# Reordering the S5 rows, dt's chain, the convolution state and GELU in a one-core decoder step

## The reference

```
xn   = rmsnorm(x)
z, xbc, dt_raw, u = split(xn @ w_in)
xbc  = silu(causal_conv4(xbc));  new conv state = last 3 input rows
dt   = softplus(dt_raw + dt_bias)
y    = SSD(xbc, dt, A) in chunks of 128;  new SSM state (16 heads x 64 x 128), per sample too
y1   = rmsnorm(y * silu(z))
s5   = diagonal complex SSM on u in 64 groups of 16 channels (state 64)
s    = gelu(s5);  y2 = rmsnorm(s * sigmoid(s @ w_glu + b))
x    = x + concat(y1, y2) @ w_out
x    = x + moe(rmsnorm(x))      # 32 experts, top 2 of one group of 8
out  = rmsnorm(x)
```

## Time and profile before

| | us |
|---|---|
| median of 3 runs | 1015.04 (1013.79 to 1019.23) |
| the profiled execution | 1019.88 |
| its span | 1018.0 |
| TensorE busy | 922.2 (91%) |
| VectorE busy | 491.6 (48%) |
| ScalarE busy | 306.4 (30%) |
| GpSimd busy | 227.7 (22%) |

### The profile page before, as it was taken

How to read it: one execution, slowest core, us unless ns; L and a number is a source line. 1 busy time by engine, 2 the same in 40 slices (tenths; PEclk the granted TensorE clock), 3 DMA queues, 4 the chain that set the end, 5 groups by cost and what they waited for, 6 DMA issues and landing times.

```text
span 1018.0 us, 16758 instructions
## 1 busy us (share of the span) xinstructions
PE 922.2 (91%) x6345; PEld 672.0 (66%) x6345; DVE 491.6 (48%) x856; ACT 306.4 (30%) x641; POOL 227.7 (22%) x468
## 2 busy tenths in 40 slices
PE   8999999989998999999989999999999888788870
PEld 7889878878896688999864555555555444445440
DVE  6999997254545888965352222222222221221136
ACT  3025322263323776423321121212212111111224
POOL 0100788888510111000001111111111101101103
PEclk9999989899999899999999999999999999999995
DMA  7576063033359755657599999989999999999976
GB/s 280 129 144 100 22 118 101 23 106 103 117 119 238 232 186 195 214 175 266 198 405 391 423 423 426 390 329 426 424 423 425 421 427 423 422 428 421 423 295 252
DMA packets 88356, 281.56 MB, mean 277 GB/s; under 512 B 37312, under 2 KB 56720, under 8 KB 70488
## 3 DMA queue, kind: packets, MB, share of 16 engines
q1 hardware_dynamic: 77632, 253.96, 67.0%
q0 software_dynamic: 8480, 19.60, 5.9%
q10 hardware_dynamic: 2176, 7.04, 1.9%
HBM read 266.39 MB, written 23.58 MB: 285 GB/s over the span
## 4 chain that ended last, share of the span: by engine, by line
PE 58%; DMA 20%; DVE 15%; issue 3%; ACT 2%; SPq 1%; POOL 0%; POOLq 0%; ACTq 0%; DVEq 0%
DMA sb_arena<-w_up 16%; PE ps L720 16%; PE ps L974 9%; PE ps L1111 8%; PE ps L1095 8%; PE ps L1086 7%; DVE sb_arena L1517 6%; PE ps L1045 2%; DMA sb_arena<-ssm_in 2%; DVE sb_arena L1526 1%; PE ps L812 1%; DVE sb_arena L2094 1%; DVE sb_arena L1650 1%; DVE sb_arena L1642 1%; DMA sb_kxf<-x_scr,sb_tok_of 1%
## 5 line engine op out<-in xcount | busy, mean ns | idle before, releaser
L720 PE MATMUL ps<-sb_arena 128*128 128x260 f32 (+2 forms) x1152 | 269.0, 395 | 2.5 <-DVE sb_arena L1551 2.3
L720 PEld LDWEIGHTS ps<-sb_arena 128*128 128x128 f32 x1152 | 222.4, 195 | 49.5 <-issue 6.4
L1111 PE MATMUL ps<-sb_arena 128*64 128x512 f32 x544 | 127.6, 612 | 18.4 <-DVE sb_arena L2094 18.4
L1095 PE MATMUL ps<-sb_arena 128*64 128x256 f32 x1088 | 123.9, 380 | 14.1 <-DMA sb_arena<-w_up 14.1
L1086 PE MATMUL ps<-sb_arena 128*64 128x256 f32 x1088 | 123.9, 380 | 10.7 <-issue 10.7
L2090 DVE TENSOR_TENSOR sb_s5b<-sb_s5b,ps 128x256 f32<-128x256 f32 x36 | 22.4, 623 | 219.8 <-PE ps L1095 219.1
L1086 PEld LDWEIGHTS ps<-sb_arena 128*64 128x64 f32 x1088 | 83.3, 137 | 61.2 <-issue 32.5
L662 POOL DMA_INDIRECT out_scr<-sb_kxf,sb_rwc x36 | 35.7, 992 | 389.8 <-DVE sb_kxf L2107 388.9
L1095 PEld LDWEIGHTS ps<-sb_arena 128*64 128x64 f32 x1088 | 78.6, 137 | 55.6 <-DMA sb_arena<-w_up 19.6
L1491 ACT ACTIVATE sb_kxf<-ps,sb_gate_of 64x512 f32<-64x512 f32 x36 | 24.5, 682 | 264.6 <-PE ps L1111 264.5
L1111 PEld LDWEIGHTS ps<-sb_arena 128*64 128x64 f32 x544 | 37.5, 139 | 86.6 <-issue 59.9
(11 more groups left out here) (326 smaller groups left out, 1142.6 us busy)
## 6 DMA issues: line engine op xcount, KB each, us to landing
sb_arena<-w_gate SPq DMA_DIRECT2D x32, 2048.0 KB, 24.2
sb_arena<-w_up SPq DMA_DIRECT2D x31, 2048.0 KB, 27.4
sb_arena<-w_down SPq DMA_DIRECT2D x31, 2048.0 KB, 23.4
sb_arena<-wi SPq DMA_DIRECT2D x27, 512.0 KB, 4.3
sb_arena<-w_out SPq DMA_DIRECT2D x16, 512.0 KB, 4.2
sb_arena<-cs_scr ACTq DMA_DIRECT2D x4, 1024.0 KB, 4.9
sb_arena<-ssm_in POOLq DMA_DIRECT2D x8, 512.0 KB, 9.3
sb_arena<-wglu SPq DMA_DIRECT2D x8, 512.0 KB, 5.4
```

The lines of the kernel that those rows point to most:

```text
L720: last = mm(ps[:, b0 + h, 0:t1 - t0], ring[w % 3][:, k, :], src[:, k, t0:t1], start=k == 0, stop=k == KD - 1)
L1095: last = mm(ps[64 * r:64 * r + 64, 1, 0:256], xt[:, k, :], Wu[i][:, k, 256 * r:256 * r + 256], start=k == 0, stop=k == KD - 1)
L1111: last = mm(ps[64 * r:64 * r + 64, 4, :], ht[:, k % 2, 64 * (k // 2):64 * (k // 2) + 64], Wd[j][:, k, 512 * r:512 * r + 512], start=k == 0 ...
```

## The change

- `y_store`: SyncE stores the even j and the samples, a new `y_store_odd` on ScalarE the odd j, in chunk 3: half 0 ahead of segment_exp(3), half 1 behind b_tokens(3).
- GpSimd starts the loads of samples 4 to 7 only after the store of half 0 has landed, and the broadcast and the loads of samples 0 and 1 only after the store of half 1.
- wide(13) stands ahead of L795; dt's polynomial is cut into pieces with conv(5), conv(6) and conv(7) in between; ScalarE's exponentials for it come after conv_silu(3).
- `ncp` and `ncs` are copied by ScalarE in `raw_evac`, from PSUM; the DMA of both waits for raw_done.
- `bc_scr`'s store is issued after raw_evac(16). conv_silu(10) goes ahead of decays(0), conv_silu(11) ahead of segment_exp(0).
- ds (`dts`, `eA`, `xds`) is computed ahead of the S5 sample states.
- GELU of tile i waits for `xn_free` i + 1, which wide(27) gives tile by tile; tiles 0 to 3 come ahead of z_evac(27) and sample_decay(0), tiles 4 to 7 behind it.
- sample_c(0) and (1) come after st_ev of chunk 3, sample_update(0) and (1) ahead of the masks of chunk 4, sample_c(2) to (5) after them.

```
             def y_store(half):
                 sp.wait_ge(y5_ev, 8 * half + 8)
                 gs = slice(32 * half, 32 * half + 32)
-                for j in range(J):
+                for j in range(0, J, 2):
                     sp.dma_start(ydst[j][:, gs], Ug[16 * j:16 * j + 16, gs, 0:NC5]).then_inc(y5_st[half], 16)
...
             pl.wait_ge(y5_mm, 8)
+            pl.wait_ge(y5_st[0], 16 * 9)
             for b in range(4, NS):
                 pl.dma_start(h0b[b], hin[b]).then_inc(h0s_ld[1], 16)
...
             pl.wait_ge(s5_out, 32)
+            pl.wait_ge(y5_st[1], 16 * 9)
             pl.dma_start(bcf, bc_scr.rearrange("b c -> (b c)").partition_broadcast(P)).then_inc(bc_ld, 16)
...
             pl.wait_ge(h0s_ld[0], 32)
-            pl.wait_ge(y5_st[1], 16 * 9)
...
+                    if w == 27 and k < KD - 1:
+                        last.then_inc(xn_free, 1)
...
             wide(12)
+            wide(13)
             pe.wait_ge(dt_ev, 1)
...
             last.then_inc(dtt_mm, 1)
-            wide(13)
             wide(14)
...
                 sm = dst[:, 531:563].rearrange("p (b j) -> p b j", j=CONV)
-                act_(sm[:, :, 3], ps[:, b0 + 1, SPLIT:N - SPLIT], ACT.Copy).then_inc(wide_free[w % 2], 1)
+                act_(sm[:, :, 3], ps[:, b0 + 1, SPLIT:N - SPLIT], ACT.Copy)
                 f = conv_tile(i)
+                act_(ncp[:, f, :], ps[:, b0 + 1, SPLIT - 3:SPLIT], ACT.Copy)
+                act_(ncs[:, f], ps[:, b0 + 1, SPLIT:N - SPLIT], ACT.Copy).then_inc(wide_free[w % 2], 1)
...
             conv_silu(9)
+            conv_silu(10)
             decays(0)
+            conv_silu(11)
...
             segment_exp(0)
-            conv_silu(XBC - 2)
-            conv_silu(XBC - 1)
...
+            def y_store_odd(half):
+                ac.wait_ge(y5_ev, 8 * half + 8)
+                gs = slice(32 * half, 32 * half + 32)
+                for j in range(1, J, 2):
+                    ac.dma_start(ydst[j][:, gs], Ug[16 * j:16 * j + 16, gs, 0:NC5]).then_inc(y5_st[half], 16)
...
             for c in range(4):
+                if c == 3:
+                    y_store_odd(0)
                 if c:
                     segment_exp(c)
                 b_tokens(c)
+                if c == 3:
+                    y_store_odd(1)
                 ac.wait_ge(l_exp, 4 * c + 4)
                 spread(c + 1)
...
-            sample_decay(0)
-            sample_decay(1)
-            z_evac(27)
-            b_tokens(4)
-            segment_exp(4)
-            for i in range(8):
...
+            for i in range(4):
+                gelu(i)
+            z_evac(27)
+            sample_decay(0)
+            for i in range(4, 8):
+                gelu(i)
+            sample_decay(1)
+            b_tokens(4)
+            segment_exp(4)
...
-            for m in (15, 13, 11, 9, 7, 5, 3):
+            for m in (15, 13):
                 tt(sp_u, sp_u, spz, ALU.mult)
                 ts(sp_u, sp_u, 1.0 / m, None, ALU.add)
+            conv(6)
+            for m in (11, 9, 7, 5, 3):
+                tt(sp_u, sp_u, spz, ALU.mult)
+                ts(sp_u, sp_u, 1.0 / m, None, ALU.add)
+            conv(7)
...
+                if c == 4:
+                    for b in range(2):
+                        sample_update(b)
                 for g in range(2):
                     dv.wait_ge(l_exp, 4 * c + 2 * g + 2)
...
-                for b in ((), (), (), (0, 1), (2, 3, 4, 5))[c]:
-                    sample_c(b)
+                if c == 4:
+                    for b in range(2, 6):
+                        sample_c(b)
                 dv.wait_ge(y_mm, c + 1)
...
                 if c == 3:
                     for b in range(2):
-                        sample_update(b)
+                        sample_c(b)
```

More of the change, by code:

```diff
@@ L306, in build @@
         raw_done, conv_done, silu_done = sem("raw_done"), sem("conv_done"), sem("silu_done")
-        h_done, sst_done, y5_mm, y5_ev = sem("h_done"), sem("sst_done"), sem("y5_mm"), sem("y5_ev")
+        xn_free = sem("xn_free")
+        h_done, y5_mm, y5_ev = sem("h_done"), sem("y5_mm"), sem("y5_ev")
         y5_st = [sem(f"y5_st{i}") for i in range(2)]
@@ L356, in build @@
         NW = 36
+        ydst = y_scr[:, 0:NP_].rearrange("(g c) (j m) -> j c g m", c=C5, j=J)
+        ysdst = y_scr[:, NP_:N].rearrange("(g c) b -> c g b", c=C5)
         def wide_bank(w):
@@ L439, in _ @@
                 ring_load(w)
-            sp.wait_ge(conv_done, XBC)
+            sp.wait_ge(raw_done, XBC)
             sp.dma_start(a["o_conv_p"].rearrange("p (k j) -> p k j", k=XBC), ncp[:]).then_inc(outs, 16)
@@ L1223, in _ @@
             conv_silu(2)
+            raw_evac(13)
+            conv_silu(3)
             ac.wait_ge(s5_dve, 3)
@@ L1234, in _ @@
             raw_evac(15)
+            conv_silu(5)
+            raw_evac(16)
             ac.wait_ge(bcs_ev, 2)
             ac.dma_start(bc_scr, btf[16:24]).then_inc(bc_st, 16)
-            conv_silu(5)
-            raw_evac(16)
             conv_silu(6)
@@ L1319, in _, with gelu @@
                         decays(c + 1)
-            sample_decay(0)
-            sample_decay(1)
-            z_evac(27)
-            b_tokens(4)
-            segment_exp(4)
-            for i in range(8):
+            def gelu(i):
                 if i % 4 == 0:
                     ac.wait_ge(yraw_ld[i // 4], 16)
+                if i < 7:
+                    ac.wait_ge(xn_free, i + 1)
+                else:
+                    ac.wait_ge(wide_done, 28)
                 act_(yg[:, i, META:NP_].rearrange("p (m j) -> p j m", j=J),
@@ L1669, in conv @@
                     stt(dst[:, 0:NP_], src[:, k:k + NP_], w_[k], dst[:, 0:NP_], ALU.mult, ALU.add)
-                    stt(dst[:, NP_:N], sm[:, :, k], w_[k], dst[:, NP_:N], ALU.mult, ALU.add)
-                link(V.tensor_copy(ncp[:, f, :], src[:, NP_:NP_ + 3]))
-                V.tensor_copy(ncs[:, f], sm[:, :, 3]).then_inc(conv_done, 1)
+                    last = V.scalar_tensor_tensor(dst[:, NP_:N], sm[:, :, k], w_[k], dst[:, NP_:N], ALU.mult, ALU.add)
+                    if k < CONV - 1:
+                        link(last)
+                last.then_inc(conv_done, 1)
             for s_ in range(2):
@@ L1698, in _ @@
             V.tensor_tensor(sp_u, sp_u, dvf, ALU.min).then_inc(s5_dve, 1)
+            conv(5)
             dv.wait_ge(s5_act, 5)
@@ L1739, in _ @@
                 conv(i)
+            dv.wait_ge(ds_mm, 1)
+            link(V.tensor_copy(dts[:], ps[:, 6, 256:256 + 64].rearrange("p (i b) -> p i b", i=8)))
+            tt(eA[:], dts[:], bc(aexp[:], 2, NS), ALU.mult)
+            ts(eA[:], eA[:], -1.0, None, ALU.mult)
+            dv.wait_ge(silu_done, XBC)
+            V.tensor_tensor(xds[:], dts[:], xcX[:, :, NP_:N], ALU.mult).then_inc(ds_ev, 1)
             lo, hi = slice(0, 64), slice(64, 128)
@@ L1748, in _ @@
             tt(smp[hi], bc(Aj[lo, 1, 1], 1, NS), h0v[lo], ALU.mult)
-            V.tensor_tensor(sst[:], sst[:], smp, ALU.add).then_inc(sst_done, 1)
-            dv.wait_ge(ds_mm, 1)
-            link(V.tensor_copy(dts[:], ps[:, 6, 256:256 + 64].rearrange("p (i b) -> p i b", i=8)))
-            tt(eA[:], dts[:], bc(aexp[:], 2, NS), ALU.mult)
-            ts(eA[:], eA[:], -1.0, None, ALU.mult)
-            dv.wait_ge(silu_done, XBC)
-            V.tensor_tensor(xds[:], dts[:], xcX[:, :, NP_:N], ALU.mult).then_inc(ds_ev, 1)
+            V.tensor_tensor(sst[:], sst[:], smp, ALU.add).then_inc(s5_dve, 1)
             def sample_c(b):
```

9 lines of the change are left out of this document (1 added, 8 removed).

## The result

Ten runs of the changed kernel had a median of 1024.92 us (1022.45 to 1027.65), ten of the kernel before 1017.15 (1013.79 to 1022.35): ratio 1.0073, 95% interval 1.0049 to 1.0097. The prediction, 1014 with a range of 1003 to 1022, was wrong. The profiled execution took 1022.66, with a span of 1020.9 (before 1019.9 and 1018.0). The forecast stood on 1015.04, the median of three runs; ten gave 1017.15, so 2.1 of the 10.9 us between forecast and result are the base.

What follows compares the result with a forecast made beforehand. TensorE's waits ahead of the expert phase and slow clock behind them, at most some 21 us, were taken as the bound. 0.0 - 3.4 + 2.5 + 0.0 = -0.9, put on the median 1015.04: 1014; range 1003 to 1022, eight in ten.

Steps and rivals of the forecast that it cites:

- (a): dt in pieces, wide(13) ahead of the dt products: dt wait goes, wide(16) waits 3.0; 0.0 us, ends -2.5 and +0.8.
- the signs: For (a): L795 without a wait, a new wait of 2 to 3.5 us before wide(16), released by the weight load.
- (d): The rest: ncp and ncs copies on ScalarE, earlier convolution outputs, ScalarE's store issues; together 0.0 us.
- (b): ds before S5 sample states, two SiLUs earlier: ds wait goes, 2.1 us wait before wide(21); -3.4 us, between -5.1 and -1.7.
- (c): S5 rows, GELU, sample states: the 4.9 us wait only moves into wide(28); +2.5 us, ends -7.7 and +8.6.
- Y: Time when all S5 stores have landed, after which POOL issues broadcast and first state loads: 322.5 us, was 335.
- The first states behind Y: POOL's broadcast and two loads, issued at Y, take 14 us and land at 336.5, between 328.5 and 341.
- Behind the fifth tile of wide(28): Extra time in the last chunk: 1.5 us for slow clock, 0.5 for wide(34)'s bank freed late.
- R2: Slower: POOL's broadcast behind the second half bounds the fifth tile of wide(28); +7.7 us in all, 1023; chance 0.15.
- R3: ScalarE sits in store issues, spread(4) lands at 330, z_evac(27) at 340; +4, so +2.9 in all, 1018; chance 0.10.

Runs made afterwards that it cites:

- e12: The changed kernel with (a) and (b) taken back, (c) and (d) kept: 1031.34 us, ratio 1.0143 to the kernel before.
- e2: The changed kernel with GELU 4 to 7 ahead of sample_decay(0) on ScalarE: 1023.93 us, ratio 1.0087 to the kernel before.
- e6: e5 with POOL's loads of states 4 to 7 behind the stores of half 1: 1009.49 us, ratio 0.9931 to the kernel before.
- e11: e6 with SyncE alone issuing all S5 stores, ScalarE none: 1012.27 us, ratio 0.9940 to the kernel before.
- e1: The changed kernel with (c) taken back, (a), (b) and (d) kept: 1011.18 us, ratio 0.9956 to the kernel before.
- e10: e6 with z_evac(20) alone ahead of segment_exp(0): 1012.86 us, ratio 0.9944 to the kernel before.
- e3: The changed kernel with spread(4) ahead of the second four stores on ScalarE: 1024.33 us, ratio 1.0093 to the kernel before.
- e4: The changed kernel with POOL's order as before, broadcast and states 0 and 1 not waiting for the stores: 1017.84 us, ratio 1.0026.
- e5: The changed kernel with the edits of e3 and e4 together: 1010.73 us, ratio 0.9936 to the kernel before.
- e9: e8 with ScalarE's wait for bcs_ev and its bc_scr store behind the sixteen evacuations of the lower-triangle products: 1015.8 us, ratio 0.9982.
- e13: e9 with ssd_c(2) ahead of all S5 output products: 1002.3 us, ratio 0.9862 to the kernel before.
- the kernel with more of the front: e1 with wide(16)'s weight load ahead of the last Toeplitz copies and z_evac(20) ahead of segment_exp(0): 1021.02 us, ratio 1.0036.
- e8: e6 with wide(16)'s weight load ahead of the last Toeplitz copies and z_evac(20) ahead of segment_exp(0): 1020.46 us, ratio 1.0027.

## Why the prediction was wrong, step by step

**(a), dt in pieces: the signs came, the cause is in part (d).** The wait at dt went, and one of 2.05 us came before wide(16), released by the weight load as named; 3.0 was forecast. From the blocks ahead of the raw dt (109.64 and 110.69) to the lower-triangle products the kernel now takes 58.4 us against 60.0, so 1.6 gained, between the ends of the range (-2.5 and +0.8), against 0.0 taken: the new wait is 1 us shorter, and the clock fell behind it for about 3.4 us instead of 6.8. But e12 shows that (d) alone takes the wait at dt away, with 56.7 us for the same stretch. Against that the kernels with (a) take 56.1 to 57.2 where the clock stayed full behind wide(16)'s wait (e2 to e6, e11), and 58.3 to 58.8 where it fell (e1, the changed kernel, e10): on top of (d), (a) is worth nothing that can be told.

**(b), ds earlier: right in mechanism.** The wait of 4.2 went and one of 1.83 was born before wide(21), released by z_evac(20); forecast 2.1. Between the lower-triangle products and wide(21) 5.3 us were gained, and 1.2 more inside wide(21), at 7.25 instead of 8.47. That is 6.5 in the profile against -3.4. The clock stayed full in the gap, which is the end named as -5.1; the other 1.4 are luck, the shorter stretch of slow clock near 190 us, which the step does not touch. Over many runs (a), (b) and (d) together gave -4.5 (the interval of e1 is -7.3 to -1.6); forecast -3.4.

**(c) is the step that failed**: +2.5 forecast, +12 measured (the changed kernel against e1), and 13.4 us in the profile; e12, with (d) in it, lies 14.5 above the kernel before (10 to 19). On the axis of the forecast, that is with 9.2 us added to the times after, three terms were off.
- Y, the end of all S5 stores: forecast 322.5, 17.3 behind the last S5 sum (305.2). Measured 316.5 behind 295.9, 20.6: 3.3 later. The store of half 0 was part of it, landed at 304.8 instead of 303.
- The first states behind Y: 14 taken, 18.5 at the upper end. Measured 18.1: 4.1 later. The 18.5 was the landing time of the kernel before; I had taken less because the stores would be over by then. They were, and the loads took as long all the same: a broadcast of 2.1 MB and two loads of 0.5 MB issued at 317 to 319.5 land at 334.5 beside y_load(1) and two weight loads. In these 18 us the queues moved 5.3 MB; at the prediction's own 3.2 us per MB that is an estimate of 17. The 10.1 us of the forecast counted the three loads of POOL alone, and 14 left 4 us for 2.1 MB more.
- Behind the fifth tile of wide(28): forecast 2.0 more than before (1.5 for the clock, 0.5 for a bank). Measured 64.3 us to the first output product against 58.5, so 5.8, 3.8 more than taken: the lower clock inside wide(28), and again from 356.5 to 363, with no wait of TensorE in the rows. What made the clock fall there is open.

The first two make 7.4, and the fifth tile of wide(28) stood at 340.6 + 9.2 = 349.8 against a forecast of 342.8. With the third the 10.9 us between +2.5 and +13.4 are accounted for. The first two are R2, to which I gave 0.15: place, releaser and condition are its own (loads of 18 us, or y5_st[1] at 326 or later; it came at 325.7), sample 0 came at 343.8 (341 to 344), and its 1023 is 2 below the median.

**R3's mechanism was there too.** z_evac(27) came at 334.3 on the forecast's axis, 2 behind "hidden behind (c) only", and left 6.2 us of wait. I had set R2 and R3 against each other with a chance each. They are two guards in series: e2 and e3 each took one away and gained nothing, e4 uncovered 10.5 us of the second, e5 took both and gained 1.4%.

**(d)** was put at 0.0, with VectorE called idle there. It was not idle ahead of dt_ev: (a) counts the copies' 0.4 us for the Toeplitz clearing, but nowhere for dt_ev, which stands behind four convolutions. e12, which has (d) and neither (a) nor (b), reaches wide(26) 2.7 us earlier than the kernel before. That is one execution, and no run takes (d) away from the changed kernel.

**The sum.** That -4.5 + 12 makes +7.5 against +7.4 measured (0.73% of 1017) is no test, since the 12 is the changed kernel less e1. The test is e12: 93.0 us from wide(26) to the first output product without (c) (the kernel before, e1), 106.4 and 106.5 with it (the changed kernel, e12), whatever the front did. What was wrong most was the size of (c) and the chance that went with it, not the bound; the front came out near its forecast with (a) and (d) wrongly shared. (R3's +2.9 should be 3.1 by the prediction's own terms; nothing rests on it.) The part's own idea, stores on two queues and GELU tile by tile, is worth little even when both chains are out of the way: 0.9931 and 0.9936 against the 0.9956 of the front alone, with overlapping intervals. Its other half, the states behind the stores, is one of the two chains that cost and is taken back in these runs.

**What the prediction did not see** at all is POOL's scan. In the kernel before the first S5 product starts 13.5 us behind its end (282.1 and 268.6), so no wait named it. It caps what the front can give at about 13 us, as long as the S5 products stand where they do.

## What to carry to other kernels

When a wait is taken away, list every chain that joins at the next place, with the time at which each would be ready, and not only the one that is last: two late chains in series make single experiments look like nothing and the pair look large. For each engine that has slack today, write down how much (here POOL's scan, 13.5 us), since a gain upstream is paid out only until that is used. When several parts go in together, run each alone, the one priced at nothing too: here it did the work that was credited to another. An engine that issues many small stores, or waits for another ahead of one, should not be the one that empties the banks of a string of small products.

## What the runs showed of the hardware that was not expected

- A wait of 1.8 us in a string of small products (75 columns) was followed by 34 us at the lower level, with TensorE busy in all 28 us of the rows from 172 to 200 (clock 0.50); the clock came back among wide products, after 200. The waits of 2.05 us before wide(16) and 1.83 before wide(21), with blocks of 264 and 260 columns behind them, cost 1.7 us (9.14 against 7.49 for a block without a wait) and nothing (7.25). The length of the wait does not decide it: before wide(16), waits of 1.93 (e1) and 2.41 us (e10) left a block of 9.18 us behind them, and one of 2.50 us (e6) a block of 7.49. The Trainium skill (TensorE: Matmul & The Clock Gate, "What's actually happening") says that the throttled state is the default and activity releases it. The trace agrees for the wide blocks; behind a wait in front of small products it did not in these rows: in e9, behind 5.2 us, the clock stood at 0.50 from 272 to 290 with TensorE busy all the time. Nor did every such wait bring the clock down: 64 of these products took 12.54 us behind a wait of 1.51 (e10), and 8.56, full clock, behind one of 1.91 (e2). A wait of 0.68 us ahead of 128 such products left them at full clock (16.91 us, 0.13 each; e13).
- POOL's scan instructions follow each other faster while VectorE is idle: 26 in 10 us with VectorE at 0.00 (180 to 190 in the kernel with more of the front), 17 in 8 us with VectorE busy for 4.7 (202 to 210 in the one without the wait in the small products), so 0.38 and 0.47 us each. That it is VectorE that holds them was not tried.
- The second four stores took ScalarE 6.9 to 8.4 us to issue where POOL's loads wait for the stores (the changed kernel, e2, e3, e12), and 9.2 to 12.6 where the broadcast and the first states are loaded beside them (e4 to e6, e8 to e10, e13).
